# Filter layer, normalised x and router logits of a two-block transformer kernel, put in another order

## The reference, cut to what matters

```
hn = rmsnorm(x, attn_norm_g);  proj = hn @ w_in            # 1024 -> 3072
hid = sin(freq * (z @ w1 + b1));  hid = sin(freq * (hid @ w2 + b2))
h = (hid @ w3) * decay  ->  filters k,  k / sum|k|,  k_freq = rfft(k)
hy = gated long convolutions of proj[:, :1536] with k_freq
at = differential attention on the rest of proj (4 heads)
x = x + concat(hy, at) @ w_out
h = rmsnorm(x, ffn_norm_g)
aff = softmax(h @ w_router)                                # 256 tokens x 16 experts
g, idx = top_k(aff.T, 32)                                  # each expert picks 32 tokens
out[idx] += g * (silu(h[idx] @ wg) * (h[idx] @ wu)) @ wd   # 16 experts, 553 MB of weights
```

## Time and profile before

| | us |
|---|---|
| median of 3 runs | 2549.59 |
| lowest, highest | 2549.44, 2549.83 |
| profiled execution, its own time | 2549.77 |
| its span, first to last instruction | 2547.8 |
| TensorE busy | 2046.3 (80%) |
| VectorE, ScalarE, GpSimd busy | 857.8, 695.5, 202.7 |
| chain that ended last | PE 46%, DMA 42%, DVE 5% |

### The profile page before, as it was taken

The page is one execution under the profiler, slowest core; times in us unless marked ns, Lnnn a source line. Parts: engine busy times, 40 slices in busy tenths (PEclk is TensorE's granted clock), DMA queues, the critical chain, the costliest instruction groups (busy, mean ns, idle before and its releaser), DMA issues.

```text
span 2547.8 us, 33989 instructions
## 1 busy us (share of the span) xinstructions
PE 2046.3 (80%) x14136; PEld 1334.8 (52%) x14136; DVE 857.8 (34%) x1503; ACT 695.5 (27%) x1230; POOL 202.7 (8%) x227
## 2 busy tenths in 40 slices
PE   9998666565666665665567699999999999999999
PEld 7655222221222222222223388886888888877887
DVE  7442000000000000000000177583665665665565
ACT  5423000000000000000000055443554655544544
POOL 2100000000000000000000087000000000250000
PEclk9999777777777677777778899999999999999999
DMA  5259999999999999999999945532655354333550
GB/s 236 96 234 382 429 430 430 430 430 430 430 430 430 430 430 430 430 430 430 431 431 430 426 169 179 192 125 90 274 194 190 149 188 172 129 141 136 186 185 18
DMA packets 53135, 753.67 MB, mean 296 GB/s; under 512 B 6848, under 2 KB 6976, under 8 KB 14400
## 3 DMA queue, kind: packets, MB, share of 16 engines
q1 hardware_dynamic: 51616, 750.33, 71.3%
q10 hardware_dynamic: 1440, 2.23, 0.3%
HBM read 751.50 MB, written 1.05 MB: 295 GB/s over the span
## 4 chain that ended last, share of the span: by engine, by line
PE 46%; DMA 42%; DVE 5%; PEldq 2%; ACT 2%; issue 1%; PEld 1%; POOL 1%; POOLq 0%; ACTq 0%; SPq 0%; DVEq 0%
DMA work<-in_expert_w 41%; PE ps L1734 13%; PE ps L1745 9%; PE ps L1736 7%; PE ps L1384 3%; PE ps L2428 2%; DMA spare<-in_ffn_w 2%; PEldq L1418 2%; PE ps L2600 1%; PE ps L488 1%; PE ps L2194 1%; PE ps L1065 1%; PE ps L1085 1%; PE ps L1679 1%; PEld ps L1412 1%
## 5 line engine op out<-in xcount | busy, mean ns | idle before, releaser
L1384 PE MATMUL ps<-ring,arena 128*32 128x352 f32 x2880 | 351.0, 651 | 227.7 <-DMA ring<-in_expert_w 227.2
L1734 PE MATMUL ps<-hsplit,w 128*128 128x512 f32 x1408 | 500.8, 398 | 0.0
L1736 PE MATMUL ps<-hsplit,w 128*128 128x256 f32 x1408 | 395.2, 281 | 0.0
L1384 PEld LDWEIGHTS ps<-ring,arena 128*32 128x32 f32 x2880 | 111.0, 144 | 463.6 <-DMA ring<-in_expert_w 299.8
L1432 ACT ACTIVATE arena<-ps 128x352 f32<-128x352 f32 x32 | 13.1, 461 | 1116.5 <-PE ps L1384 1116.5
L1734 PEld LDWEIGHTS ps<-hsplit,w 128*128 128x128 f32 x1408 | 264.6, 188 | 64.6
L1444 DVE TENSOR_TENSOR arena<-arena,ps 128x352 f32<-128x352 f32 x32 | 15.2, 516 | 762.2 <-ACT arena L1432 762.2
L1736 PEld LDWEIGHTS ps<-hsplit,w 128*128 128x128 f32 x1408 | 265.9, 189 | 3.1
L1745 PE MATMUL ps<-w,hidsplit 128*128 128x512 f32 x1056 | 255.6, 391 | 0.1
L1783 DVE TENSOR_TENSOR w<-ring,w 128x1024 fp32r<-128x1024 f32 x168 | 213.4, 1272 | 26.9 <-ACT w L1779 26.5
L1745 PEld LDWEIGHTS ps<-w,hidsplit 128*128 128x128 f32 x1056 | 192.0, 188 | 41.2 <-issue 0.5
(11 more groups left out here) (481 smaller groups left out, 2483.0 us busy)
## 6 DMA issues: line engine op xcount, KB each, us to landing
ring<-in_expert_w SPq DMA_DIRECT2D x126, 2816.0 KB, 35.7
work<-in_expert_w SPq DMA_DIRECT2D x64, 2816.0 KB, 35.7
ring<-in_ffn_w SPq DMA_DIRECT2D x87, 1536.0 KB, 6.8
ring<-in_w_in_tiles SPq DMA_DIRECT2D x7, 1536.0 KB, 14.1
ring<-in_s_slots SPq DMA_DIRECT2D x6, 1536.0 KB, 6.7
ring<-in_ple_w_gate SPq DMA_DIRECT2D x4, 1536.0 KB, 6.5
ring<-in_c_w SPq DMA_DIRECT2D x4, 1536.0 KB, 6.8
early<-in_expert_w SPq DMA_DIRECT2D x2, 2816.0 KB, 14.8
```

Source lines behind the costliest of these rows:

```text
L1384: last = pe.matmul(k.ps[32 * g:32 * g + CAP, 2 * w + half, 0:FH], k.xfirst[:, kk, :] if first_one else xe[:, kk, :], weights[:, at:at + FH ...
L1734: pe.matmul(k.ps[:, bank(c, w), :], k.w13[:, b, w, 0, kk, :], k.hsplit[:, :, kk, :], start=(kk == 0), stop=False, skip_group_check=True)
L1736: last = pe.matmul(k.ps[:, bank(c, w), 0:S], k.w13[:, b, w, 1, kk, :], k.hsplit[:, 0, kk, :], start=False, stop=(kk == DK - 1), skip_group ...
```

## The change

1. TensorE runs 12 instead of 15 dummy matmuls, and the filter's first layer stands behind the eighth instead of the twelfth.
2. ScalarE scales the first tile of x (new, with its own semaphore `scale_ready`), VectorE the second alone.
3. ScalarE splits column blocks 0 and 1 of `w_in` ahead of the transposed x, VectorE forms the remainder of block 0 ahead of it. `sine(0)` comes directly behind the split x.
4. `second_layer` and `layer_arg(1)` stand behind column 0 instead of 1, `sine(1)` behind 3 instead of 4, and the tables for taps, magnitudes, frequencies, folds and sums are all two columns earlier.
5. Router logits are formed as tokens by experts: 128 tokens of x are stationary and the router's 16 columns move. The copy and the turning back are gone. The scaled logit is formed with the sign reversed, so that the minimum is what the exponential needs as bias.
6. The first round of maxima reads PSUM; the copy of the affinities is gone.

```
-TAPS_AT = {6: (0,), 7: (1, 2), 8: (3, 4), 9: (5, 6), 10: (7,)}
+TAPS_AT = {4: (0,), 5: (1, 2), 6: (3, 4), 7: (5, 6), 8: (7,)}
-MAGNITUDES_AT = {10: 0, 11: 1}
+MAGNITUDES_AT = {8: 0, 9: 1}
...
-WARM = 15
+WARM = 12
+FIRST_LAYER_AT = 8
@@ prologue, tensor
         for n in range(WARM):
-            if n == WARM - 3:
+            if n == FIRST_LAYER_AT:
                 first_layer()
...
-            if c == 1:
+            if c == 0:
                 second_layer()
@@ prologue, scalar
+        act.wait_ge(scale_ready, 1)
+        act.activation(b.xn[:, 0, :], k.x[:, 0, :], ACT.Copy, scale=stat[:, 4:5]).then_inc(normed, 1)
         high(0)
+        high(1)
         for i, kk in enumerate(KK_ORDER):
...
-        for c in range(1, AHEAD):
+        sine(0)
+        for c in range(2, AHEAD):
             high(c)
-            if c == 1:
-                sine(0)
...
-            if c == 4:
+            if c == 3:
                 sine(1)
@@ prologue, vector
-        step(dve.reciprocal(stat[:, 4:6], stat[:, 2:4]))
-        dve.wait_ge(x_loaded, 16)
-        for ti in range(ST):
-            dve.tensor_scalar(b.xn[:, ti, :], k.x[:, ti, :], stat[:, 4 + ti:5 + ti], None, ALU.mult).then_inc(normed, 1)
+        dve.reciprocal(stat[:, 4:6], stat[:, 2:4]).then_inc(scale_ready, 1)
+        dve.wait_ge(scale_ready, 1)
+        dve.tensor_scalar(b.xn[:, 1, :], k.x[:, 1, :], stat[:, 5:6], None, ALU.mult).then_inc(normed, 1)
+        low(0)
...
-            if i == 1:
-                low(0)
...
-            if c == 1:
+            if c == 0:
                 layer_arg(1)
@@ routing, tensor
-                last = pe.matmul(k.ps[0:NE, 0, t * P:(t + 1) * P], wr[:, kk, :], k.hT[:, kk, t * P:(t + 1) * P],
+                last = pe.matmul(k.ps[:, 1, t * NE:(t + 1) * NE], k.hT[:, kk, t * P:(t + 1) * P], wr[:, kk, :],
                                  start=(kk == 0), stop=(kk == DK - 1))
         last.then_inc(logits_done, 1)
+        keep_busy(k, pe, 7, 5)
         pe.wait_ge(aff_ready, 2)
-        for t in range(ST):
-            last = pe.transpose(k.ps[:, 1, t * NE:(t + 1) * NE], logitT[0:NE, t * P:(t + 1) * P], k.ident[0:NE, 0:NE])
-        last.then_inc(aff_turned, 1)
-        keep_busy(k, pe, 7, 5)
-        pe.wait_ge(aff_ready, 3)
@@ routing, scalar
-            act.activation(aff[:, t, :], logit[:, t, :], ACT.Exp, bias=m[:, 6 + t:7 + t],
+            act.activation(aff[:, t, :], logit[:, t, :], ACT.Exp, scale=-1.0, bias=m[:, 6 + t:7 + t],
@@ routing, vector
-        dve.tensor_copy(logitT[0:NE, :], k.ps[0:NE, 0, 0:S]).then_inc(aff_ready, 1)
-        dve.wait_ge(aff_turned, 1)
         dve.wait_ge(r_ready, 1)
-        step(dve.tensor_tensor(logit, k.ps[:, 1, 0:ST * NE].rearrange("p (t e) -> p t e", t=ST),
-                               m[:, 4:6].unsqueeze(2).to_broadcast([P, ST, NE]), ALU.mult))
-        step(dve.tensor_reduce(m[:, 6:8], logit, AX, ALU.max))
-        dve.tensor_scalar(m[:, 6:8], m[:, 6:8], -1.0, None, ALU.mult).then_inc(exp_arg, 1)
+        step(dve.scalar_tensor_tensor(out=logit, in0=k.ps[:, 1, 0:ST * NE].rearrange("p (t e) -> p t e", t=ST), scalar=-1.0,
+                                      in1=m[:, 4:6].unsqueeze(2).to_broadcast([P, ST, NE]), op0=ALU.mult, op1=ALU.mult))
+        dve.tensor_reduce(m[:, 6:8], logit, AX, ALU.min).then_inc(exp_arg, 1)
...
-        step(dve.tensor_copy(left[0:NE, :], k.ps[0:NE, 2, 0:S]))
         for r in range(CAP // 8):
-            step(dve.max(top[0:NE, 8 * r:8 * r + 8], left[0:NE, :]))
+            values = left[0:NE, :] if r else k.ps[0:NE, 2, 0:S]
+            step(dve.max(top[0:NE, 8 * r:8 * r + 8], values))
             step(dve.match_replace(out=left[0:NE, :], in_to_replace=top[0:NE, 8 * r:8 * r + 8],
-                                   in_values=left[0:NE, :], imm_value=-1.0))
+                                   in_values=values, imm_value=-1.0))
```

More of the change, by code:

```diff
@@ L380, in prologue_buffers @@
     return b
-TAPS_AT = {6: (0,), 7: (1, 2), 8: (3, 4), 9: (5, 6), 10: (7,)}
+TAPS_AT = {4: (0,), 5: (1, 2), 6: (3, 4), 7: (5, 6), 8: (7,)}
 TAP_ORDER = [(_ti, _n) for _n in range(2 * NORD) for _ti in range(ST)]
-MAGNITUDES_AT = {10: 0, 11: 1}
-FREQS_AT = {11: (0, 1, 2), 12: (3, 4, 5), 13: (6, 7), 14: (8, 9)}
-FOLDS_AT = {11: (0, 0), 12: (0, 1), 13: (1, 0), 14: (1, 1)}
-SUMS_AT = {15: (0, 1)}
+MAGNITUDES_AT = {8: 0, 9: 1}
+FREQS_AT = {9: (0, 1, 2), 10: (3, 4, 5), 11: (6, 7), 12: (8, 9)}
+FOLDS_AT = {9: (0, 0), 10: (0, 1), 11: (1, 0), 12: (1, 1)}
+SUMS_AT = {13: (0, 1)}
 FREQS = NORD * (FM + 1)
@@ L410, in prologue @@
     taps_ready, taps_put, abs_done, l1_done = sem("taps_ready"), sem("taps_put"), sem("abs_done"), sem("l1_done")
+    scale_ready = sem("scale_ready")
     freq_ready, freq_put, hT_bank = sem("freq_ready"), sem("freq_put"), sem("hT_bank")
@@ L985, in vector @@
                 magnitude(MAGNITUDES_AT[c])
-            if c == 16:
+            if c == 14:
                 dve.wait_ge(l1_done, NORD)
@@ L1114, in routing @@
     aff = area(k, 6304, 32, t=ST)
-    logitT = area(k, 6336, 256)
     left = area(k, 6592, 256)
@@ L1262, in vector @@
         dve.tensor_tensor(aff, aff, m[:, 8:10].unsqueeze(2).to_broadcast([P, ST, NE]), ALU.mult).then_inc(aff_ready, 1)
-        dve.wait_ge(aff_turned, 2)
-        step(dve.tensor_copy(left[0:NE, :], k.ps[0:NE, 2, 0:S]))
+        dve.wait_ge(aff_turned, 1)
         for r in range(CAP // 8):
-            step(dve.max(top[0:NE, 8 * r:8 * r + 8], left[0:NE, :]))
+            values = left[0:NE, :] if r else k.ps[0:NE, 2, 0:S]
+            step(dve.max(top[0:NE, 8 * r:8 * r + 8], values))
             step(dve.match_replace(out=left[0:NE, :], in_to_replace=top[0:NE, 8 * r:8 * r + 8],
-                                   in_values=left[0:NE, :], imm_value=-1.0))
+                                   in_values=values, imm_value=-1.0))
         step(dve.tensor_scalar(left[0:NE, :], left[0:NE, :], 0.0, None, ALU.is_lt))
```

## The result

The changed kernel took 2556.34 us in the median of 11 runs (2553.95 to 2558.15), the kernel before 2549.72 in the median of 11 runs beside it (2548.76 to 2552.69): a ratio of 1.0024 with a 95% interval of 1.0015 to 1.0032, which is clear of no change. A second set of 11 runs, beside 33 others of the kernel before, gave 2554.33 against 2550.14, 1.0017 (1.0008 to 1.0026); brackets behind a ratio give its 95% interval from here on. The forecast was 2551.0, its range ended at 2554.0: the prediction was wrong. The profiled execution took 2556.73, with a span of 2554.9 against 2547.8.

A forecast was written before the change was run, and what follows sets the result against it. The expert-weight stream, its DMA full, starts when routing frees the first tile, so prologue and routing microseconds count one to one. +0.7 + 0.9 + 1.2 - 1.4 = +1.4 gave 2551.0 us; range 2547.3 to 2554.0.

The forecast's parts named there:

- Start and first tap: Prologue to first tap: column 1 begins 2.4 sooner, but TensorE waits 4.4 for the sines; +0.7, bounds -3.3 and +1.7.
- Second wait: Before the sixth frequency product: VectorE's chain has one convolution more, +0.9, bounds 0 and 1.9.
- Clock in the prologue: Behind the 4.4 wait before the first tap: one added fall of TensorE's clock, +1.2, bounds 0 and 2.9.
- Rival (3): Prologue: the clock's fall at 101.6 may not come, 1.7 less, so -0.3 in all and 2549.3; chance 0.12.
- Rival (2): From the first tap on: three further clock falls of 1.7 each, +5.3, 2554.9 (with two 2553.2); chance 0.05.
- Routing, -1.4: Router to first expert product: exp starts directly behind its table load and a copy goes, -1.4, bounds -1.7 and -0.5.
- Behind the expert weights: After the eighth expert piece's issue: nothing changes, so the end moves by as much as that issue.

The follow-up runs named there:

- tables alone: Kernel before with only part 4 (second layer, second argument, sines one column sooner, all tables two columns sooner): 2556.36 us, 1.0019.
- start alone: Kernel before with only parts 1 to 3, taps and tables as before: 2547.63 us, 0.9989; second set 2548.20, 0.9991.
- the delay: Kernel before with 26 instead of 15 dummies in front of the first layer, nothing else: 2555.63 us, 1.0018.
- few dummies: Changed kernel without the routing's first dummies (ten passes) and with 12 instead of 24 passes in the second group: 2552.69 us, 1.0010.
- the routing part: Kernel before with only parts 5 and 6: 2551.17 us, 0.9999; run again 2552.73, 1.0006.

## Why the prediction was wrong

Its sum was +0.7 + 0.9 + 1.2 - 1.4 = +1.4; the profile shows +7.1, of which 3.8 are the prologue (forecast 2.8), 1.05 the routing (-1.4) and 2.3 the handover (nothing).

- Start and first tap, +0.7: right. The tap at 32.17 with two columns behind it is +0.72, and the mechanism (the start's gain of 2.4 eaten by the wait for the sines) was shown by start and tables alone. In the start alone the first tap came 3.0 sooner, 34.16 against 37.14: the 2.4, and the 0.54 of waiting that it no longer had. The first argument came 1.5 sooner and not 1.9 (by three dummies in 1.56, four would even be 2.1); later steps made up for that.
- Second wait, +0.9: right, 4.40 against 3.49.
- Clock in the prologue, +1.2: mechanism right, size off in this profile. Behind the first tap up to the next tap products it cost 2.35 (the tap 2.05 instead of 1.10, column 5 4.25 instead of 2.85), at the sixth frequency another 1.27 over what it had cost before, and the fall at 101.6 did not come, -1.56: +2.06. Rival (3) and the first half of Rival (2) came in together. The missing third fall goes with the new tables: none of the seven profiles that have them shows a fall from 76 to 190, while the ten with old tables and without the delay all have one, at 101.6 or at 155 to 161; why is open. The size, though, is one execution's: in the six profiles with the changed prologue the pair stood 1.87 to 3.80 later than in the profile before. The 2.8 that the prediction gives to the prologue lies within that.
- **Routing, -1.4: this is the step that failed; it was +1.05.** The part that was reasoned from rows held: without a fall it was -1.55, and -1.36 with a fall once the dummies were few. What failed are two sentences. "No row has this form, and I take the same 3.67, bounds -0.5 and +1" bounded the products' own duration, which was kept (4.34), and forgot what they do to the clock. "TensorE's five dummies ... end at about 197.1, just before they would be in the way" had a margin of some 0.3 at full clock; they were moved to directly behind the logits, and at the lower clock they took 2.2 more. The cover of a wait was reckoned at one clock only, though the page before showed two falls within the first 105 us.
- Behind the expert weights, nothing: +2.3 in this profile. The kernel before had been profiled in an execution with full clock there, which 12 of 18 had not. This part of the miss is bad luck and says nothing about the change.

The Trainium skill (TensorE: Matmul & The Clock Gate, section on HAM oscillation) reckons the loss as half of the throttled time. The stretch behind the first tap agrees: 2.35 lost in some 5 at half clock. By it the prediction would have put the fall that it added at 1.7 and not at 1.2, closer to the 2.06. In the routing the runs do not: with the same clock of 0.74 in the stretch it cost 0.2 with few dummies (18.50 against 18.30) and 2.6 with all (20.90), since TensorE is the bound there only as far as its dummies make it so.

The range failed with the terms: all three misses went the same way, and the far case of Rival (2), 2554.9, was given 0.05. How far it failed is in part chance: the first runs are 2.3 above its end, the second set, 2554.33, only 0.3.

## What to carry to other kernels

Dummies that fill a wait have to end in time at the lower clock too: halve their number, or ask what waits for the instruction behind them if they take twice as long. A product with few moving columns behind which dummies stand is to be priced at both clocks. When work is pulled ahead of another engine's chain, look first at what that chain needs: here the taps had to wait for the sines, and the start alone, with the taps left where they were, gained 3.2 and 2.1 in its two sets of runs, more than any other part of the change. And where single executions differ by falls of the clock, compare the distances between fixed places of several profiles, not one span with another.

## What the hardware showed unexpectedly

- The form of a matrix product bears on the clock. With 128 columns stationary and 16 moving, the 32 passes of the router stand as busy as before in the records (3.64 against 3.67 at full clock), and the clock fell under them in 6 of 9 profiles and in the wait behind them in 2 more; with 16 stationary and 128 moving it did so in none of 9. Why is not shown.
- Whether a given fall comes, and how long it lasts, differs between executions of one kernel. At 101.6 it came in one of the four profiles with the old prologue, while the other three had one at 158 to 161; under the router it came in one of the two profiles of the routing part, at the handover in one of the two of the start alone and in 12 of all 18. Single profiles differ by 1 to 3 us by it, and the 33 times of the kernel before in the first set go from 2548.79 to 2554.30.
- A maximum of eight over 16 x 256 took 0.42 from PSUM, as long as from SBUF.
